# A delta-rule scan on one core: three steps in the pipeline, and the inverse turned in 32x32 blocks by VectorE

## The reference

```python
xm = jnp.where(strict, jnp.einsum('bnhik,bnhjk->bnhij', kb, kc) * decay, 0.0)
tm = lax.linalg.triangular_solve(xm + eye, ..., left_side=True, lower=True, unit_diagonal=True)
u = jnp.einsum('bnhij,bnhjv->bnhiv', tm, vc * bc[..., None])
w = jnp.einsum('bnhij,bnhjk->bnhik', tm, kb * jnp.exp(gc)[..., None])
attn = jnp.einsum('bnhik,bnhjk->bnhij', qc, kc) * decay
def step(s, inp):
    u_i, w_i, a_i, qg_i, ke_i, ge_i = inp
    v_new = u_i - jnp.einsum('bhlk,bhkv->bhlv', w_i, s)
    o_i = jnp.einsum('bhlk,bhkv->bhlv', qg_i, s) + jnp.einsum('bhij,bhjv->bhiv', a_i, v_new)
    s = s * ge_i[..., None, None] + jnp.einsum('bhlk,bhlv->bhkv', ke_i, v_new)
    return s, o_i
```

## Time and profile before

| | us |
|---|---|
| median of 3 runs | 4317.01 (4314.04 to 4319.1) |
| the profiled execution's own time | 4315.75 |
| its span, first to last instruction | 4314.1 |
| TensorE busy | 3852.5 (89%) |
| VectorE busy | 1490.1 (35%) |
| ScalarE busy | 704.1 (16%) |
| GpSimd busy | 457.0 (11%) |

### The profile page before, as it was taken

The page is one execution under the profiler, slowest core; times in us unless marked ns, Lnnn a source line. Parts: engine busy times, 40 slices in busy tenths (PEclk is TensorE's granted clock), DMA queues, the critical chain, the costliest instruction groups (busy, mean ns, idle before and its releaser), DMA issues. The chain is left out here.

```text
span 4314.1 us, 52664 instructions
## 1 busy us (share of the span) xinstructions
PE 3852.5 (89%) x22122; PEld 2171.5 (50%) x22122; DVE 1490.1 (35%) x2543; ACT 704.1 (16%) x1416; POOL 457.0 (11%) x521
## 2 busy tenths in 40 slices
PE   4999989978689999999999988999568999677995
PEld 1444478864334444444444446444447888333442
DVE  4656279973510000000000005550564555231003
ACT  1000022211110001000100003221253333011111
POOL 0000000002000000000000002000214555200110
PEclk8999999989889999999999999999789999798998
DMA  6566323214188888888888855221120000318995
GB/s 264 200 242 236 131 117 137 98 52 188 54 325 308 309 308 310 306 309 307 309 308 309 300 182 217 85 72 61 66 73 3 4 4 4 134 59 314 343 333 182
DMA packets 283551, 815.81 MB, mean 189 GB/s; under 512 B 10945, under 2 KB 18425, under 8 KB 268118
## 3 DMA queue, kind: packets, MB, share of 16 engines
q1 hardware_dynamic: 263066, 720.11, 46.3%
q0 software_dynamic: 19168, 82.08, 5.8%
q10 hardware_dynamic: 1116, 10.71, 0.6%
HBM read 718.21 MB, written 94.66 MB: 188 GB/s over the span
## 5 line engine op out<-in xcount | busy, mean ns | idle before, releaser
L1285 PE MATMUL banks<-moe_ring,moe_xeT 128*128 128x512 f32 x2560 | 1129.6, 595 | 6.9 <-ACT moe_xeT L1326 6.9
L1285 PEld LDWEIGHTS banks<-moe_ring,moe_xeT 128*128 128x128 f32 x2560 | 482.7, 191 | 583.6 <-issue 580.8
L1271 PE MATMUL banks<-moe_ring,moe_hidT 128*128 128x512 f32 x1280 | 562.7, 593 | 1.7 <-DVE moe_ye L1365 1.0
L1379 DVE TENSOR_TENSOR moe_hid<-moe_silu,banks 128x512 f32<-128x512 f32 x80 | 55.0, 688 | 1429.1 <-PE banks L1285 1429.1
L1271 PEld LDWEIGHTS banks<-moe_ring,moe_hidT 128*128 128x128 f32 x1280 | 241.1, 190 | 293.1 <-issue 290.9
L1594 PE MATMUL banks<-hT,w_in_ring 128*128 128x512 f32 (+3 forms) x976 | 362.3, 533 | 1.7 <-ACT hT L1666 0.9
L434 PE MATMUL banks<-hT,w_in_ring 128*128 128x512 f32 x768 | 341.8, 600 | 3.8 <-ACT hT L456 3.8
L1594 PEld LDWEIGHTS banks<-hT,w_in_ring 128*128 128x128 f32 (+1 forms) x976 | 182.2, 187 | 179.9 <-issue 170.1
L1345 ACT ACTIVATE moe_silu<-banks 128x512 f32<-128x512 f32 x80 | 47.8, 597 | 1302.8 <-PE banks L1285 1302.8
L434 PEld LDWEIGHTS banks<-hT,w_in_ring 128*128 128x128 f32 x768 | 143.5, 191 | 193.7 <-issue 180.1
L969 PE MATMUL banks<-w_out,mix 128*128 128x512 f32 x512 | 226.5, 601 | 7.0 <-DMA w_out<-d_w_out 5.4
(11 more groups left out here) (429 smaller groups left out, 4160.9 us busy)
## 6 DMA issues: line engine op xcount, KB each, us to landing
moe_ring<-d_wg SPq DMA_DIRECT2D x80, 2048.0 KB, 8.4
moe_ring<-d_wu SPq DMA_DIRECT2D x80, 2048.0 KB, 8.3
moe_ring<-d_wd SPq DMA_DIRECT2D x80, 2048.0 KB, 8.0
x_normed<-d_ada_w SPq DMA_DIRECT2D x12, 2048.0 KB, 12.1
w_in_ring<-d_w_in SPq DMA_DIRECT2D x9, 2048.0 KB, 11.2
x_normed<-d_mod_w SPq DMA_DIRECT2D x8, 2048.0 KB, 14.3
d_taps<-dft SPq DMA_DIRECT2D x8, 2048.0 KB, 7.4
taps_in<-d_taps SPq DMA_DIRECT2D x8, 2048.0 KB, 9.4
```

Source lines behind the costliest of these rows:

```text
L1271: last = nc.tensor.matmul(m.ps[:, Y_BANK + h, :], hidT[:, c, i * P:(i + 1) * P], down(c)[:, i, h * BANK:(h + 1) * BANK], start=(fc == 0 an ...
L1285: last = nc.tensor.matmul(m.ps[:, 2 * kind + c, :], xeT[:, k, :], up(c, kind)[:, k, :], start=(k == 0), stop=(k == KT - 1))
L1379: nc.vector.tensor_tensor(hid[:, j % 2, :], sg[:, j % 2, :], m.ps[:, 2 + j % 2, :], ALU.mult).then_inc(s.hid, 1)
```

## The change

The loop gets one iteration more (21), and iteration c works on three steps: the levels of step c, the state chain of step c - 1 (`before`), and the front of step c + 1 (`after`). Buffers that live longer get more copies: attention and k_to_end three (`RING`), the level masks and both inverses two.

The flips on TensorE are gone. VectorE turns the inverse with `nc.vector.transpose`, which turns each 32x32 block in its place (up to level 4 the inverse is zero outside its diagonal 32x32 blocks): `first_level` turns inverse_t into the inverse, `level` turns the inverse after each of the levels 1 to 4. k_to_end and the new values are made by ScalarE, in three scaled copies a lane, where VectorE made them. Keys x keys, keys x queries and the turned keys share the front's bank, one after the other. The first eight latent chunks of each direction are written to the output tile directly; the zeros that were put there at the start are gone, and only the last eight add (`joined`).

TensorE's new order, and the new operations:

```diff
-            def flipped(d, out, left):
-                return each(d, out, left, lambda p: t.tab[:, EYE, :])
+            for c in range(N_STEPS + 1):
+                if n:
+                    level_product(n, 1)
+                if before:
+                    state_products(before)
+                if n:
+                    level_change(n, 1)
+                if after:
+                    decays(after)
+                if n:
+                    level_product(n, 2)
+                    level_change(n, 2)
+                if before:
+                    new_values(before)
+                if n:
+                    level_product(n, 3)
+                if after:
+                    key_products(after)
+                if n:
+                    level_change(n, 3)
+                if before:
+                    state_change(before)
+                if n:
+                    level_product(n, 4)
+                if after:
+                    query_products(after)
+                if n:
+                    level_change(n, 4)
+                if lat:
+                    attended(before)
+                if n:
+                    level_product(n, 5)
+                if after:
+                    keys_turned(after)
+                if n:
+                    level_change(n, 5)
...
+            def keys_to_end(n):
+                for d in LANES:
+                    act.wait_ge(L.kt_mm, n.at(1, 1))
+                    for p in range(PAIRS):
+                        last = nc.scalar.activation(kend[:, n.c % RING, d, p, :], front(d)[:, p, :], ACT.Copy,
+                                                    scale=now(n, d, TO_END)[:, p:p + 1])
+                    last.then_inc(L.ke, 1)
...
+            for c in range(N_STEPS + 1):      # ScalarE
+                    products_out(n, 1)
+                    products_out(n, 2)
+                    pair_decays(after)
+                    products_out(n, 3)
+                    new_values(Step(c - 1))
+                    products_out(n, 4)
+                    products_out(n, 5)
+                    keys_to_end(after)
...
+            for c in range(N_STEPS):          # GpSimd
+                masked(Step(c))
+                if c + 1 < N_STEPS:
+                    steps_in(Step(c + 1))
+                levels(Step(c))
+                if c + 1 < N_STEPS:
+                    betas_in(Step(c + 1))
...
+            def turned(out, of):
+                return nc.vector.transpose(out.rearrange("p k c -> p (k c)"), of.rearrange("p k c -> p (k c)"))
+            def first_level(n):
+                for d in LANES:
+                    v.wait_ge(L.tt0, n.at(1, 1))
+                    turned(inv[:, n.par, d], invt[:, n.par, d]).then_inc(L.t, 1)
+            def level(n, l):
+                for d in LANES:
+                    v.wait_ge(L.t_mm, n.at(4, l))
+                    nc.vector.tensor_tensor(inv[:, n.par, d], inv[:, n.par, d], change(d), ALU.subtract).then_inc(L.t, 1)
+                for d in LANES:
+                    v.wait_ge(L.t, n.at(5, l + 1))
+                    turned(invt[:, n.par, d], inv[:, n.par, d]).then_inc(L.tt, 1)
...
+            for c in range(N_STEPS + 1):      # VectorE
+                    state_read(before, 0)
+                    level(n, 1)
+                    state_read(before, 1)
+                    rest(before)
+                    level(n, 2)
+                    decayed(before)
+                    matrix(after)
+                    level(n, 3)
+                    state(before)
+                    attention(after)
+                    level(n, 4)
+                    out(before)
+                    joined(before)            # in the second half of the latent steps
+                    last_level(n)
+                    first_level(after)
```

More of the change, by code:

```diff
@@ L2438, in step @@
-                    if lat:
-                        last = each(d, second(d), lambda p: queries(n, d, p), lambda p: t.state[:, d, p, :])
+                        last = each(second(d), lambda p: queries(n, d, p), lambda p: t.state[:, d, p, :])
                     last.then_inc(L.p_mm, 1)
[L2441 to L2466, removed]
@@ L2467, in step, with new_values @@
-                for d in range(2):
+            def new_values(n):
+                for d in LANES:
                     L = lanes[d]
@@ L2477, in step, with state_change @@
+            def state_change(n):
+                for d in LANES:
                     L = lanes[d]
                     pe.wait_ge(L.vn, n.at(1, 1))
[L2479 to L2491, removed]
+                    pe.wait_ge(L.ke, n.at(1, 1))
+                    each(second(d), lambda p: kend[:, n.c % RING, d, p, :], lambda p: vn[:, d, p, :]).then_inc(L.s_mm, 1)
+            def attended(n):
+                for d in LANES:
+                    L = lanes[d]
+                    pe.wait_ge(L.st, n.at(1, 2))
+                    each(first(d), lambda p: attn[:, n.c % RING, d, p, :], lambda p: vn[:, d, p, :]).then_inc(L.av_mm, 1)
@@ new lines, in products_out, with new_values @@
+            def products_out(n, l):
+                for d in LANES:
+                    L = lanes[d]
+                    act.wait_ge(L.a_mm, n.at(5, l))
+                    nc.scalar.copy(a_[:, d], product(d)).then_inc(L.a, 1)
+            def new_values(n):
+                for d in LANES:
+                    L = lanes[d]
+                    act.wait_ge(L.vn_mm, n.at(1, 1))
+                    for p in range(PAIRS):
+                        last = nc.scalar.activation(vn[:, d, p, :], first(d)[:, p, :], ACT.Copy, scale=now(n, d, BETA)[:, p:p + 1])
+                    last.then_inc(L.vn, 1)
@@ new lines, in last_level, with state_read @@
+            def last_level(n):
+                for d in LANES:
+                    L = lanes[d]
+                    v.wait_ge(L.last_mm, n.at(1, 1))
+                    v.wait_ge(L.tt, n.at(4, 4))
+                    nc.vector.tensor_tensor(invt[:, n.par, d], invt[:, n.par, d], change(d), ALU.subtract).then_inc(L.last, 1)
+            def state_read(n, d):
+                L = lanes[d]
+                decay = wide(now(n, d, FROM_START))
+                v.wait_ge(L.p_mm, n.at(1, 1))
+                if d == 0 and lat_of(n.c) > LAT_CHUNKS // 2:
+                    st.wait()
+                st.did(nc.vector.tensor_tensor(r[:, d], first(d), decay, ALU.mult))
+                if n.c >= CTX_STEPS:
+                    nc.vector.tensor_tensor(o1[:, d], second(d), decay, ALU.mult).then_inc(L.o1, 1)
@@ new lines, in joined @@
+            def joined(n):
+                j = lat_of(n.c)
+                for d in LANES:
+                    L = lanes[d]
+                    at = LAT_CHUNKS - 1 - j if d else j
+                    v.wait_ge(L.o, j + 1)
+                    st.did(nc.vector.tensor_tensor(t.out[:, at], t.out[:, at], o1[:, d], ALU.add))
+            for d in LANES:
+                nc.vector.memset(t.state[:, d], 0.0).then_inc(lanes[d].st, 1)
+            matrix(Step(0))
+            attention(Step(0))
+            first_level(Step(0))
```

320 lines of the change are left out of this document (173 added, 147 removed).

## The result

The changed kernel takes 4223.96 us (median of 4 runs, 4223.15 to 4225.86) against 4316.58 us (4 runs, 4314.04 to 4319.1): a ratio of 0.9787, 95% interval 0.9775 to 0.9799, 92.6 us less. The forecast was 4214 in a range of 4192 to 4262, so direction and range held and the time was 10 us more than forecast. Its profiled execution took 4224.36 us, its span is 4222.7.

What follows compares the result with a forecast made beforehand. TensorE was taken as nearest to a bound in the scan. Prologue 8.3, first iteration 13.7, 4 x 13.6, 8 x 14.7, 7 x 14.95 and tail 6.1 made 304.8 us against 407.8, 103 less: 4214 us, range 4192 to 4262.

Steps and rivals of the forecast that it cites:

- The mechanism: Delta-rule scan: other steps' work covers most level links; TensorE's 13.3 us of work plus small waits makes 14.7 us a latent step.
- a period near 14.8 in the second half: Sign that the forecast holds: the scan's step period in its second half would be near 14.8 us.
- The turn: VectorE's 128x192 transpose of the inverse, 10 a step, priced at 0.38 us each with no overlap.
- rival 2: A VectorE turn runs at RECIPROCAL's rate, 1.40 us, making 24.6 us a step and 4400 us in total; chance 0.05.
- The scaled copies: ScalarE's 12 scaled copies of 128x64 a step: 0.73 us a lane, 1.33 us for both lanes.
- The three small waits: TensorE waits 0.28 us at change 2, 0.2 at state change, 0.96 at the seam (next step's first product awaiting first_level's turn).
- The early part: Scan's start: 8.3 us until product 1, 13.7 for the first iteration, then context steps of 13.6 and latent steps of 14.7.
- the sums of the late steps: Two VectorE additions into gdn_out ahead of last_level, 607 ns each, lengthen seven steps by 0.25 us to 14.95.
- The state's decay: VectorE's two-input operation on the state meets GpSimd's masks, but what follows it on VectorE is not late.
- VectorE as the bound: Turns of about 0.6 us make VectorE the bound at 16.7 us a step, 36 us more, 4250; chance 0.17.
- rival 3: The four fixed-order queues interlock, so links counted as covered are paid: 17.3 us a step, 4262 in total; chance 0.10.
- rival 4: All waits vanish and TensorE alone bounds: 13.3 us a step, 28 us less, 4186 in total; chance 0.08.

Runs made afterwards that it cites:

- run 5: Changed kernel with the turns of levels 1 to 4 given back to TensorE and copied out by ScalarE: 4280.73 us.
- run 4: Kernel before with only its TensorE flips replaced by VectorE transposes, old order of steps kept: 4301.3 us.
- run 3: Changed kernel with the next step's first_level moved ahead of out, joined and last_level on VectorE's queue: 4196.55 us.
- run 7: Changed kernel with first_level ahead of out and last_level, and joined behind last_level: 4193.86 us.
- run 1: Changed kernel with GpSimd's level masks 2 to 5 as four 128x192 operations a lane instead of one of 128x768: 4210.06 us.
- run 2: Changed kernel with the two sums into gdn_out (joined) moved behind first_level on VectorE's queue: 4210.59 us.
- run 8: Changed kernel with first_level early, joined last, level masks 2 to 5 split, and the state's decay at the head of VectorE's iteration: 4221.13 us.
- run 9: Changed kernel with first_level early, joined last and the state's decay at the head of the iteration, masks whole: 4202.63 us.
- run 6: Changed kernel with each turn of the levels made twice, the extra one into a spare tile: 4229.33 us.
- run 10: Changed kernel with first_level early, joined last and level masks 2 to 5 split, the state's decay in its old place: 4196.57 us.

## Why the prediction was right, and by how much not

- **The mechanism** held: the links of a level are covered by the work of two other steps, and TensorE's own work sets the period. 36 groups and `decays`, 13.3 us of work, showed as 440 records and a period of 14.62 us (forecast 14.7), 13.54 with a context step behind (13.6). Run 5 puts the flips' groups back and gets their 57 us back; run 4 shows that without the pipeline they are worth a quarter of that. The sign "a period near 14.8 in the second half" held for the undisturbed steps and not for the six with the sums (16.06 to 18.05).
- **The turn** takes 352 ns, with the next 0.28 us later (two in 0.63 us); I had 0.38 without overlap. So the nearest row, the other operations of that shape, was the price, and the bound from RECIPROCAL with rival 2 was empty. By the Trainium skill ("VectorE: DVE Perf Modes", The three transpose paths) my estimate was 0.38; measured is a little less.
- **The scaled copies** take 331 ns each, six in 1.35 us; I had 1.33. The estimate from the Trainium skill ("ScalarE: Activation LUTs", What ACT_TABLE_LOAD costs), 1.5, was high by 0.15.
- **The three small waits.** At change 2 TensorE waits 0.20 (forecast 0.28), at the state change 0.13 (0.2), at the seam 0.88 (0.96). Runs 3 and 7 confirm the place of the last.
- **The early part.** The first iteration took 14.45 instead of 13.7 (its granted clock was 0.80, and 0.50 from 3266.71 to 3270.0, behind a wait of 2.84 us; the 13.7 had no term for that), the start up to product 1 7.9 instead of 8.3, four context steps 0.2 less, eight latent steps 0.2 less in all (with one stall of 0.46 included), the last iteration and the tail 21.15 instead of 21.05 (with about 1.4 us of a fallen clock in it, 0.92 on average, so the work itself was over-priced by as much). Together about 0, which is errors in both directions and so partly luck.
- **The term that was mis-sized: the sums of the late steps.** "They make the seam 0.25 late: 14.95." The six periods between the first and the last of them took 103.05 us in sum against 6 x 14.95 = 89.7, so +13.35, which is the whole excess of the stage (318.2 against 304.8). I took 607 ns for a sum from the earlier trace rows, where in the kernel before it stood beside short GpSimd operations; in the new order it stands beside the 128x768 products and takes 1273 ns in the mean. The prediction named the neighbour and kept the old price. (In the seam at 3469.30 the first sum takes 1297 ns and the second 1953; they end 0.1 to 0.2 us behind the first and the second of the two 128x768 products.) The time stayed in the forecast's own range of 4200 to 4235, but that range had been drawn for the turn's cost, not for this. Five seams of about 2.76 and one of 2.32 instead of 0.88 are 10.8 us (I had allowed 6 x 0.25); TensorE's clock, which I had left out, fell behind four of them, and three of these lie within the six periods, 3 x 1.5 = 4.5 us. Runs 1 and 2 took both away together and gave 14 back.
- **The state's decay** was named and put at nothing for TensorE. It doubled, from 351 to 695 ns in the mean, and no wait of TensorE followed. Run 8 and run 9 show what it costs in a place where one does.
- The stage's excess of 13.4 less 1.8 us that the rest of the kernel was shorter (1.3 longer ahead of the stage, 3.1 shorter behind it) is the 11.6 by which the profiled execution (4224.36) lies above 4212.8.
- **The rivals.** VectorE as the bound at 16.7 us a step: its condition, a turn of 0.6, did not occur (VectorE was busy for 11.24 of 15.02 us in a middle step and for 14.21 of 16.49 in a late one, standing included), and run 6 shows the slack. The interlock of rival 3 did not occur either. For rival 4, "It needs a cover for the seam, and there is none" was wrong: the cover was there. `first_level(after)` depends on nothing of this step's last level, it only stood behind it in the queue. With it moved up the period is 13.7 us, and run 7 at 4194 is within 8 us of that rival's 4186.

The Trainium skill ("GPSIMD Engine Reference", 1. Specifications) says that the two engines share their interfaces to SBUF for VectorE's two-input work. The runs agree, and go further than I had drawn from it: in runs 8, 9 and 10 the price is no factor on the operation, but a wait that ends with GpSimd's run of operations. In run 1 it is shorter, and what decides that is open.

## What to carry to other kernels

An operation's duration from the old trace holds for its old neighbours: when the order changes, ask of each VectorE operation with two SBUF inputs what GpSimd will be doing then, and price it by how long GpSimd stays busy, not by the operation (the most it cost here; sometimes it was less). On a queue in fixed order, look for what stands behind a wait without needing it; that was worth 27 us here. Taking work off the busiest engine pays in full only when it is bound by work and not by links: the same turns were worth 15 us in the old order and 57 in the pipeline. The waits that such a change leaves can also cost clock (some 15 us in run 4), so read the granted clock of both versions before a missing gain is put down to waits alone.

## What the runs showed of the hardware that I had not expected

- A VectorE operation with two SBUF inputs can stand until GpSimd's whole unbroken run of operations ends: one `s_decayed` took 4134 ns at the longest in run 8, against 343 at the shortest. At other times it gets in at the end of a single GpSimd operation (run 1, 346 to 744 ns). VectorE's transposes (352 ns mean of 160) and its operations with one input from PSUM (`out`, 0.33 us) are not held up beside the same GpSimd work.
- Splitting a GpSimd operation of 128x768 into four of 128x192 costs little: 0.86 us for both lanes, 3.59 to 4.45.
- A wait of TensorE of 2.8 us was followed by the lower clock for a while in some steps and not in others (behind 2.76, 2.74, 2.76 and 2.32 us it fell, behind 2.76 and 2.77 it did not), each fall about 1.5 us. In run 6 it fell behind one of six waits of 2.1 to 2.5 us, in run 4 behind waits of 1.76 us in 12 of 15 periods, for 1.0 to 1.5 us each. Where the waits were 0.9 us (runs 1 and 2) it did not fall in these steps. What decides between the like ones was not tried.
- Some steps have stalls of TensorE of 0.2 to 1.8 us for which the trace shows no releaser ("issue"): its weight loads have 1.4 us of them in the stage of the changed kernel and of run 1, 1.7 to 5.2 in the other versions with all turns on VectorE and the new order, 14.6 in run 5. They ate part of the gain of run 3. Their cause is open.
